# Opening of a two-layer hybrid backbone: the first feed-forward quad taken in two halves of the contraction, with its four weights loaded in two pairs

## The reference, cut to what matters

```python
c_act = silu(c); cc_act = silu(c_ctx)
mod  = (c_act  @ w_mod + b_mod).reshape(1, 1, 9, 1024)      # latent tokens
modc = (cc_act @ w_mod + b_mod).reshape(9, 1024)            # context tokens
ada  = lambda t, g, shift, scale: rms_norm(t, g) * (1 + scale) + shift
ffn  = lambda t, pre: (silu(t @ w_gate) * (t @ w_up)) @ w_down
x  = x  + 0.5 * m(2)  * ffn(ada(x,  norm_ffn1, m(0),  m(1)),  'ffn1')
xc = xc + 0.5 * mc(2) * ffn(ada(xc, norm_ffn1, mc(0), mc(1)), 'ffn1')
# then four token mixers, the merge, the second SwiGLU; two layers; a last norm
```

## Time and profile before

| what | value |
|---|---|
| median of 3 runs (lowest to highest) | 2163.85 us (2163.36 to 2164.53) |
| the profiled execution: its time, its span | 2162.38 us, 2160.6 us |
| TensorE busy | 2114.4 us, 98% of the span |
| VectorE, ScalarE, GpSimd busy | 1481.3, 1014.0, 615.3 us |
| granted TensorE clock, mean | 0.997 |
| share of the last-ending chain on TensorE, VectorE, ScalarE | 84%, 8%, 3% |

### The profile page before, as it was taken

One profiled execution on the slowest core, in us unless ns is written; L12 is line 12 of the kernel. 1 busy time (PEld: TensorE's weight loads), 2 busy tenths in 40 slices (PEclk: granted clock), 3 DMA queues, 4 the chain that ended last, 5 costly groups with the idle time before them and its releaser, 6 DMA issues.

```text
span 2160.6 us, 31674 instructions
## 1 busy us (share of the span) xinstructions
PE 2114.4 (98%) x11845; PEld 1776.3 (82%) x11845; DVE 1481.3 (69%) x2074; ACT 1014.0 (47%) x1589; POOL 615.3 (28%) x615
## 2 busy tenths in 40 slices
PE   7999999999999999999999999999999999999998
PEld 4878788987766778988888898888889887888997
DVE  4898898875576456877777775445457868776555
ACT  4544445554455543554344553222245556745444
POOL 1566666402000027344444420000013201261000
PEclk9999999999999999999999999999999999999999
DMA  9487686623333354655556465545545445576564
GB/s 309 133 233 200 171 217 173 190 78 97 94 114 89 90 174 134 185 167 161 156 159 177 138 185 156 150 141 157 155 127 157 118 125 154 150 207 178 184 185 137
DMA packets 471963, 340.61 MB, mean 158 GB/s; under 512 B 13226, under 2 KB 437654, under 8 KB 471686
## 3 DMA queue, kind: packets, MB, share of 16 engines
q1 hardware_dynamic: 441312, 238.06, 38.7%
q0 software_dynamic: 29056, 96.35, 15.9%
q10 hardware_dynamic: 1446, 4.20, 0.5%
HBM read 326.98 MB, written 12.36 MB: 157 GB/s over the span
## 4 chain that ended last, share of the span: by engine, by line
PE 84%; DVE 8%; issue 4%; ACT 3%; DMA 1%; POOL 0%; SPq 0%; DVEq 0%; ACTq 0%; POOLq 0%
PE bank L832 18%; PE bank L833 18%; PE bank L837 18%; PE bank L900 4%; PE bank L910 4%; PE bank L901 3%; DVE w_lo L801 3%; PE bank L984 2%; PE bank L985 2%; PE bank L990 2%; PE bank L1337 1%; PE bank L1313 1%; PE bank L1106 1%; PE bank L1105 1%; PE bank L1112 1%
## 5 line engine op out<-in xcount | busy, mean ns | idle before, releaser
L801 DVE TENSOR_TENSOR w_lo<-raw,w_hi 128x1024 fp32r<-128x1024 f32 (+1 forms) x442 | 580.9, 1316 | 472.8 <-PE bank L837 258.9
L791 ACT ACTIVATE w_hi<-raw 128x1024 fp32r<-128x1024 f32 (+1 forms) x442 | 461.6, 1044 | 590.8 <-PE bank L833 291.1
L832 PE MATMUL bank<-h_hi,w_hi 128*128 128x512 f32 (+1 forms) x1728 | 597.5, 358 | 3.0 <-DVE X L2028 1.5
L833 PE MATMUL bank<-h_lo,w_hi 128*128 128x512 f32 (+1 forms) x1728 | 592.0, 355 | 0.0
L832 PEld LDWEIGHTS bank<-h_hi,w_hi 128*128 128x128 f32 x1728 | 326.5, 189 | 52.6 <-issue 4.4
L837 PE MATMUL bank<-h_hi,w_lo 128*128 128x512 f32 (+1 forms) x1728 | 367.1, 355 | 0.0
L833 PEld LDWEIGHTS bank<-h_lo,w_hi 128*128 128x128 f32 x1728 | 326.6, 189 | 46.3 <-issue 1.0
L837 PEld LDWEIGHTS bank<-h_hi,w_lo 128*128 128x128 f32 x1728 | 291.5, 189 | 45.5
L832 PE MATMUL bank<-inner_hi,w_hi 128*128 128x256 f32 (+1 forms) x654 | 205.5, 336 | 2.5 <-DVE X L2028 2.5
L833 PE MATMUL bank<-inner_lo,w_hi 128*128 128x256 f32 (+1 forms) x654 | 204.4, 334 | 0.0
L2452 POOL DMA_DIRECT2D wm<-in_w_mod_dram x128 | 92.6, 724 | 361.9 <-DVE gstage L2000 158.0
(11 more groups left out here) (300 smaller groups left out, 3448.8 us busy)
## 6 DMA issues: line engine op xcount, KB each, us to landing
wm<-in_w_mod_dram POOLq DMA_DIRECT2D x128, 512.0 KB, 4.4
raw<-in_w_in_dram SPq DMA_DIRECT2D x108, 512.0 KB, 4.1
raw<-in_ffn_w_down_dram SPq DMA_DIRECT2D x94, 512.0 KB, 4.1
raw<-in_ffn_w_gate_dram SPq DMA_DIRECT2D x88, 512.0 KB, 4.5
raw<-in_ffn_w_up_dram SPq DMA_DIRECT2D x88, 512.0 KB, 4.2
raw<-in_w_out_dram SPq DMA_DIRECT2D x24, 512.0 KB, 3.9
raw<-in_ffn_w_down_dram SPq DMA_DIRECT2D x24, 384.0 KB, 3.9
raw<-in_w_branch_dram SPq DMA_DIRECT2D x16, 512.0 KB, 4.3
```

The lines of the kernel that those rows point to most:

```text
L791: act.activation(w_hi[w_slot[n]][:, 0:unit.rows, :], raw[unit.slot][:, 0:unit.rows, :], ACT.Copy).then_inc(hi_made, 1)
L801: dve.tensor_tensor(w_lo[w_slot[n]][:, 0:unit.rows, :], raw[unit.slot][:, 0:unit.rows, :], w_hi[w_slot[n]][:, 0:unit.rows, :].bitcast(F32) ...
L832: pe.matmul(psum, w_hi[s][:, k, :], hi, start=(k == 0), stop=False)
L833: mm = pe.matmul(psum, w_hi[s][:, k, :], lo, start=False, stop=False)
```

## The change

- **Feature halves.** The 16 pieces are taken in the order of `MOD_ORDER`: shift of blocks 0 to 3, scale of blocks 0 to 3, shift of blocks 4 to 7, scale of blocks 4 to 7. `opening_vectors(0)` makes the vectors of blocks 0 to 3 after 8 pieces, `opening_vectors(1)` the others after 16.
- **Loads.** SP sends pieces 0 to 7, w0, w1, pieces 8 to 15, w2, w3. Pieces no longer use the `raw` slots; 13 to 15 go to `x_in`, whose tokens are transposed by then. The small parameter loads of `pack2` move from ScalarE's queue to GpSimd's.
- **The quad.** `opening_quad` works on 512 columns at once. Blocks 0 to 3 are staggered by one block per unit, and the last 8 pieces and the third turn are put between its steps; after the fourth turn, blocks 4 to 7 run with the four units side by side.
- **The norm.** Both streams of a block are normed together. On ScalarE the splits of w2 and w3 stand behind blocks 0 and 1.
- **The tokens.** TensorE transposes each token half as it lands, VectorE copies (before: ScalarE), ScalarE squares. The eight filling matmuls of `run_on` are gone. VectorE's eight `skip_w` copies move behind the norm.

```diff
+MOD_ORDER = (0, DC, DC // 2, DC + DC // 2)
@@ SP
                     for j in range(MOD_FIRST):
-                        if j >= 14:
-                            sp.wait_ge(unit_done, j - 14 + 8 + 1)
+                        if j == MOD_FIRST // 2:
+                            for p in range(2):
+                                load(first["up", 0, 1, 0] + p, 0, (0, 0), ...)
+                        if 10 <= j < 13:
+                            sp.wait_ge(unit_done, j - 6 + 1)
+                        if j == 13:
+                            pe_start.wait(sp, ("x", 7))
                         mod_loaded[j].done(sp.dma_start(mod_rows(j), ...))
+                    for p in range(2, 4):
+                        load(first["up", 0, 1, 0] + p, 0, (0, 0), ...)
@@ PE
+            def opening_step(u, which, k):
+                if which == 0:
+                    for st in range(2):
+                        h_made.wait(pe, (0, 1, k, st))
+                if k == 0:
+                    pe.wait_ge(hi_made, units[u].product + 1)
+                pe.matmul(psum, w_hi[s][:, k, :], hi, start=(k == 0), stop=False)
+                mm = pe.matmul(psum, w_hi[s][:, k, :], lo, start=False, stop=False)
+                if k == DC - 1:
+                    mm.then_inc(hi_used, 1)
+                if k == 0:
+                    pe.wait_ge(lo_made, units[u].product + 1)
+                mm = pe.matmul(psum, w_lo[s][:, k, :], hi, start=False, stop=(k == DC - 1))
+            def opening_quad(u0):
+                for step in range(HALF + 3):
+                    for which in range(4):
+                        if 0 <= step - which < HALF:
+                            opening_step(u0 + which, which, step - which)
+                    if step in LATE_PIECES:
+                        i, j = LATE_PIECES[step]
+                        modulation(i, j)
+                        modulation(i, j + 1)
+                    if step == LATE_TURN:
+                        turn_modulation(2)
+                turn_modulation(3)
+                for k in range(HALF, DC):
+                    for which in range(4):
+                        opening_step(u0 + which, which, k)
-            def run_on(times):
@@ ACT
                     for s in range(2):
                         split_hi(act, s)
+                    vectors.wait(act, (0, "in", 0))
+                    for k in range(HALF):
+                        for st in range(2):
+                            norm_hi((0, 1), k, st)
+                        if k in (0, 1):
+                            split_hi(act, 2 + k)
+                    for i in range(2, 4):
+                        copy_modulation(i)
                     vectors.wait(act, (0, "in"))
-                    for st in range(2):
-                        for k in range(DC):
+                    for k in range(HALF, DC):
+                        for st in range(2):
                             norm_hi((0, 1), k, st)
@@ DVE
+                    opening_vectors(0)
+                    for k in range(HALF):
+                        for st in range(2):
+                            norm_scale((0, 1), k, st)
+                        for st in range(2):
+                            norm_lo((0, 1), k, st)
+                        split_lo(dve, k)
+                    opening_vectors(1)
...
```

More of the change, by code:

```diff
@@ L952, in first_quad @@
                     last = st == streams(n)[-1]
-                    if key == (0, 1) and st == 0:
-                        pe.wait_ge(lo_made, units[u0].product + 1)
-                        pair_pass(range(u0, u0 + 4), st, last, bank[0:4], (0, 2, 4, 6), key)
-                        continue
                     if n == LAT:
@@ L969, in pair_pass @@
                 for step in range(DC + max(behind)):
[L970 removed]
+                    if (st, step) == (0, 4) and banks[0] is bank[0] and key != (LAYERS - 1, 2):
                         sum_squares(key, 1)
@@ L1005, in sum_squares, with sum_tokens, turn_tokens @@
                 sums.done(mm, (key, st))
+            def sum_tokens(st):
+                summed.wait(pe, ((0, 1), 4 * st + 3))
+                for half in range(2):
+                    mm = pe.matmul(sum_bank((0, 1), st)[:, stream_cols(st)], const("ones"), wb[:, st, stream_cols(half)],
+                                   start=(half == 0), stop=(half == 1))
+                sums.done(mm, ((0, 1), st))
+            def turn_tokens(m):
+                st, j = m // 4, m % 4
+                token_loads[st].wait(pe, "all")
+                if m >= 3:
+                    tokens_copied.wait(pe, m - 3)
+                for k in range(2):
+                    for t in range(2):
+                        mm = pe.transpose(token_bank(m)[:, k * LAT + t * P:k * LAT + (t + 1) * P],
+                                          x_in[:, 2 * st + t, (2 * j + k) * P:(2 * j + k + 1) * P], const("ident"))
+                pe_start.done(mm, ("x", m))
             def modulation(i, j):
@@ L1043, in gather_macs @@
                 mac_folded.wait(pe, g)
+                pick_loads.wait(pe, "all")
                 for q in range(4):
@@ L1237, in turn_packs @@
                 start_loads.wait(pe, "all")
+                pack2_loads.wait(pe, "all")
                 for l in range(LAYERS):
@@ L2199, in prepare @@
                     prepared.done(ins, (l, "cumtok", 0))
-            start_loads.wait(dve, "all")
-            for l in range(LAYERS):
-                for g in range(2):
-                    for half in range(2):
-                        rows = slice(half * HD, (half + 1) * HD)
-                        head = 4 * l + 2 * g + half
-                        ins = dve.tensor_copy(skip_w[rows, l, g:g + 1], skip_all[rows, head:head + 1])
-            link(ins)
             for l in range(LAYERS):
@@ L2604, in _ @@
             small_loads(0)
+            pick_loads.done(pool.dma_start(const("pick32"), consts[:, FIRST_CONSTS:LATER_CONSTS]), "all")
             accumulate(0, 1)
```

251 lines of the change are left out of this document (146 added, 105 removed).

## The result

The changed kernel takes **2180.93 us** in the median of 4 runs (2179.85 to 2182.21); the kernel before, on the same chip, 2164.19 (2163.36 to 2165.36, 4 runs). The ratio is 1.0079 with a 95% interval of 1.0064 to 1.0094: slower by 16.7 us, where the forecast was +10.4 in a range of +5 to +15.7. The direction was right, and so was the main mechanism, the wait for w2 in ScalarE's order. The size was short by 6 us, and the time lies 1.4 us outside the range.

A forecast was written before the change was run, and what follows sets the result against it. The prediction took the opening's chain, handed on when unit 0 frees its slot, as what bounds the kernel: +7.7 us there plus 2.7 for the clock gives +10.4, so 2163.85 becomes 2174.2 us; range 2169 to 2179.5 (8 in 10).

The forecast's parts named there:

- What is handed on: Opening: the moment unit 0 frees its `w_hi` slot (62.65 us before), not the quad's end, shifts the whole kernel.
- Loads: SP's queue: w2 lands at 38.9 us, between 38 and 40.3; SP's new waits cost nothing.
- the 0.6 taken off for GpSimd's loads: w2's landing: 39.5 less 0.6 us, because GpSimd's next loads come only after the fourth turn.
- The first half: Opening up to block 0: second turn ends near 25 us, unit 0's first step done near 30.
- ScalarE's wait for w2: ScalarE stands at w2's split before norming block 1; TensorE idle 11 to 12 us, block 1 ready 2.65 after w2.
- From block 1 to the slot: TensorE's quad: matmuls 21.2, late pieces 4.1, turns 2.0, block 2's wait 0.6, seam 3.2 us; clock 2.7 more.
- the 0.6 us wait: Quad: TensorE comes to block 2 at 5.1 us after w2's landing, block 2 is ready at 5.65.
- dearer: Rival: w2 at 40.3, late pieces dearer, longer clock fall; +12 to +16 us, 2176 to 2180; chance 14%.
- Late pieces at twice their price: Quad, part of the dearer rival: late pieces cost double because they alternate with products, +4.1 us at most.
- Overtaking: Wire: w2 and w3 pass the late pieces and land near 28 us; the faster rival's premise, chance 4%.
- overlap as meant: Rival: the wait for w2 does not hold block 1, so the halves overlap; +2.6 us, 2166.4; chance 7%.
- faster: Rival: w2 and w3 land near 28 us, quad ends at 57.1; -7.8 us, 2156; chance 4%.

The follow-up runs named there:

- e6: Changed kernel with blocks 4 to 7 taken in two pairs of units, (0, 1) before (2, 3): 2174.68 us, ratio 1.0048.
- e4: Changed kernel with late pieces 10 to 13 going to `x_in` and only 14 and 15 to `wm`: 2177.46 us, ratio 1.0064.
- e5: Changed kernel with TensorE's first sum of token squares later, squares in one go on ScalarE, both reciprocals at the end on VectorE: 2178.27 us.
- e13: e9 with an earlier second sum of squares, fillers before blocks 0 and 1, w2 and w3 again behind the last piece, split behind block 3: 2168.41 us.
- e1: Changed kernel with the splits of w2 and w3 moved behind the norms of blocks 0 to 3: 2175.1 us, ratio 1.0056.
- e2: Changed kernel with seven filling matmuls on TensorE behind the fourth turn, at the seam between the halves: 2177.18 us, ratio 1.0067.
- e12: Changed kernel with nine filling matmuls on TensorE behind unit 0's first step, in the first idle stretch: 2177.65 us, ratio 1.0062.
- e8: Changed kernel with the edits of e3, e5, e2 and e6 together: 2166.72 us, ratio 1.0014 to the kernel before.
- e9: e8 with e4's edit added: 2165.12 us, ratio 1.0009 to the kernel before.
- e3: Changed kernel with all four weights sent between the halves, w2 and w3 directly behind w1: 2173.01 us, ratio 1.004.

## Why the prediction was right and wrong, point by point

- **What is handed on: right.** The shift at the split (+15.11) is that at 157.76 (+15.12), and e6 moved the slot alone and moved the total. Only "from then on the same distances" was not quite so: the last 2.4 us of the profiled execution come behind it. This term, nought in the sum, lies in the stretches of the later clock falls.
- **Loads: the step that failed.** "SP's new waits ... end near 20 to 23 us, when the queue still holds several pieces, and cost nothing." They end between 25.4 and 32.2, the wire has a hole at 29 to 35, and w2 comes at 42.04 instead of 38.9: **3.1 of the 4.7 us** missing at the landmark. The waits are 1.3 to 1.9 of these: with a full wire w2 comes at 40.1 to 40.7 (e4, e5, e13). The other 1.2 to 1.8 us were missing in the sum as well: the 0.6 taken off for GpSimd's loads is not seen, and the rest has no shown cause. One place to look is the beginning, which the sum took as unchanged: by 16 us the wire has moved about 0.1 MB less in these three than in the kernel before, some 0.3 us by its 385 GB/s; the small loads that moved to GpSimd's queue are issued there, but no run tries them. The bound "40.3 (a stall somewhere in SP's queue)" allowed for one of the two shortfalls, not for both.
- **The first half: wrong by 7 us, without a price in the changed kernel.** Block 0 came at 37.09, not near 30. I charged the moved token work with nothing, under "over 10 us of slack". Two in-order waits were overlooked: TensorE at `sum_tokens(0)` for squares that VectorE adds only at 15 us (3.57), and `sum_tokens(1)` behind piece 5, on which root, reciprocal (1.75 each) and vectors hang. The slack really covered it (e5: block 0 2.9 us earlier, w2 still the one waited for), but the same lateness of TensorE made the hole above: in e5, where TensorE comes to pieces 4 to 6 earlier, the hole is gone. With block 0 only at 37.62, e1 too could win 3.1 and not more. "No price" was true of the path and false of what hung on it.
- **ScalarE's wait for w2: right** as mechanism (5.79 us idle, released by the transfer of w2) and in what follows it (2.59 for 2.65). TensorE's idle stretch was 5.8 us and not 11 to 12, because block 0 was late; the path does not see this.
- **From block 1 to the slot:** predicted 28.85 without the clock and 31.55 with it; measured 33.16. By e2 and e12 the falls cost 2.5 us at the seam and 0.9 ahead of block 1, 3.4 for 2.7: **0.7 of the missing 1.6**. I had taken 1.7 at the seam from the single fall of the earlier trace rows; half level held for 5.2 us behind the seam. The 1.0 ahead of block 1, "since part of it lies in the 0.6 us wait", was right, and for that reason. The Trainium skill, "TensorE: Matmul & The Clock Gate", Part 1: The HAM clock gate, says that the default state is throttled and that activity releases the throttle. By that rule the first idle stretch had to cost; the trace agrees (0.50 at 45 to 47 us, gone when filled in e12). The other 0.9 us are the steps themselves: at full clock block 2 to block 4 takes 17.5 us where the sum had 17.2, and block 4 to the slot 9.13 (e2) where it had 8.65, 38 times 0.2275; a product inside the quad comes every 0.23 us and the first behind a wait takes longer. The seam took 2.93 for 3.2, unit 6's wait 4.08 for "some 4". Unit 4 did not start "at once" but waited 0.78, which costs nothing on the path.
- **Rivals.** The "dearer" case is nearest to what came, by w2 later than its bound and by a longer fall, though 2180.93 lies above its 2180; its own three terms would add to +16.9, not to the +16 at which it ends. "Late pieces at twice their price" did not come (1.07 for two at full clock). "Overtaking" did not come: w2 landed behind all sixteen pieces in the changed kernel. The page "DMA: Bandwidth & Descriptors" of the Trainium skill, Queues, rings and completion order, allows a completion out of order; no run here shows one that matters. The "overlap as meant" did not come in the changed kernel. That e8 and e9 (2166.7 and 2165.1) lie near its 2166.4 says nothing for its sum, since they load and order differently. The terms of "faster" add to 56.6 and not 57.1, which changes nothing.
- **Sum:** 10.4 + 3.1 (w2, of which 1.3 to 1.9 the hole) + 0.7 (clock) + 0.9 (steps) + 2.4 (later) = 17.5, the difference of the two profiled executions; the medians differ by 16.7.

## What to carry to other kernels

A buffer reused for a transfer ties the DMA queue to the engine that empties it: find when that engine really gets there, with all the waits in its own order, before saying that "the queue still holds enough". Ask of slack not only whether the path is covered but who else is released by the same event. Before cutting a start in two, put everything that both halves need first in each engine's order, then keep TensorE busy in the gaps; here that, with all four weights between the halves and the units in pairs, turned +0.8% into about -0.1%. Read a landmark from more than one trace before you believe its last microsecond.

## What the runs showed of the hardware

- The wire carried 385 to 390 GB/s in stretches with pieces of `w_mod` (rows of 2 KB), and 289 to 301 in stretches in which the weights' [128 x 128] blocks travelled; the first read as a DMA share of 1.04 to 1.06, the second as 1.17 to 1.20: the higher share goes with fewer bytes, so the share alone does not tell how fast bytes move.
- Taking the first half earlier did not bring w2 earlier by the same amount: 2.9 us at block 0, 1.3 us at w2 (e5), the latter within the scatter of w2 between traces (41.62 to 43.14 with the hole).
- The same transfer takes a different time in each execution: the 1 MB of latent tokens, issued at 1.2 us with the same loads around it, landed 5.0 to 7.2 us later in the traces of the changed kernel and its twelve versions (5.0 in e3, 7.2 in e13), and what follows starts that much later.
- After an idle stretch of 2.9 us TensorE ran at half level for 5.2 us of work (66.1 to 71.3); filled, it kept its level. Work at half level looks normal in the busy share: 1.00 in each of these windows. Only the duration of a product (0.43 for 0.23 us) or the clock column shows it.
- Where ScalarE waits for unit 0's slot in the changed kernel, the chain of waits gives 6.62 us as "issue" (71.17 to 77.79), with no releaser. That it is the slot had to be read from the ten matmuls that still follow (77.79 + 10 x 0.23 = 80.1, the quad's end) and was shown by e6.
